# A two-layer transformer trunk: one more Strassen block in the last FFN, and six adaLN sums moved into FoX's head steps

## What is computed

```python
c_act = silu(c)
for i in range(2):
    mod = c_act @ ada_w[i] + ada_b[i]
    sh_a, sc_a, g_a, sh_f, sc_f, g_f = split(mod, 6)
    h = x * (1 + sc_a) + sh_a
    y = mla(h) if i == 0 else fox(h)           # 16 heads each, output projection w_o
    x = layer_norm(ALPHA * x + (1 + g_a) * y)
    h = x * (1 + sc_f) + sh_f
    y = (silu(h @ w1[i]) * (h @ w3[i])) @ w2[i]
    x = layer_norm(ALPHA * x + (1 + g_f) * y)
```

## Time and profile before

| | us |
|---|---|
| median of 3 runs | 2184.3 (2183.52 to 2187.05) |
| the profiled execution | 2183.23 |
| its span, first to last instruction | 2181.5 |
| PE busy | 2130.8 (98%) |
| DVE busy | 1677.3 (77%) |
| ACT busy | 1024.9 (47%) |
| mean granted clock of TensorE | 0.997 |

### The profile page before, as it was taken

The page is one execution under the profiler, slowest core; times in us unless marked ns, Lnnn a source line. Parts: engine busy times, 40 slices in busy tenths (PEclk is TensorE's granted clock), DMA queues, the critical chain, the costliest instruction groups (busy, mean ns, idle before and its releaser), DMA issues.

```text
span 2181.5 us, 25010 instructions
## 1 busy us (share of the span) xinstructions
PE 2130.8 (98%) x9515; PEld 1737.1 (80%) x9515; DVE 1677.3 (77%) x1868; ACT 1024.9 (47%) x1334; POOL 105.1 (5%) x208
## 2 busy tenths in 40 slices
PE   5799999999999999999999999999999999999999
PEld 2378877888888888888788888878888888888887
DVE  6789989787777777778887566878787755787766
ACT  1077636544443444443544454554445534465543
POOL 2101100000000000000000000000000000000000
PEclk9999999999999999999999999999999999999999
DMA  9999997789998898999678778958985765576672
GB/s 388 418 363 365 360 391 271 283 296 336 338 338 328 322 337 323 325 332 366 216 270 329 258 270 288 343 178 267 348 301 206 277 230 175 162 257 217 223 281 85
DMA packets 177065, 635.90 MB, mean 291 GB/s; under 512 B 20385, under 2 KB 51377, under 8 KB 150705
## 3 DMA queue, kind: packets, MB, share of 16 engines
q1 hardware_dynamic: 147298, 427.93, 54.6%
q0 software_dynamic: 27792, 201.34, 24.7%
q10 hardware_dynamic: 1856, 5.04, 0.6%
HBM read 616.37 MB, written 17.86 MB: 291 GB/s over the span
## 4 chain that ended last, share of the span: by engine, by line
PE 87%; DVE 6%; DMA 5%; ACT 1%; issue 1%; POOL 0%; ACTq 0%; SPq 0%; DVEq 0%; POOLq 0%
PE ps L2106 45%; PE ps L2112 22%; PE ps L2409 7%; PE ps L2415 3%; PE ps L2123 3%; DMA gate<-in_ada_w 3%; PE ps L2391 2%; DMA raw<-in_mla_w_o 1%; DVE wlo L1356 1%; PE ps L2396 1%; DMA ada_head<-in_ada_w 1%; DVE ada_w L1393 1%; DVE gate L1393 1%; DMA ada_w<-in_ada_w 1%; PE ps L2335 0%
## 5 line engine op out<-in xcount | busy, mean ns | idle before, releaser
L850 ACT ACTIVATE whi<-raw 128x1024 fp32r<-128x1024 f32 (+1 forms) x645 | 679.0, 1056 | 852.6 <-PE ps L2112 698.4
L1356 DVE TENSOR_TENSOR wlo<-raw,whi 128x1024 fp32r<-128x1024 f32 (+1 forms) x645 | 777.2, 1214 | 356.2 <-ACT whi L850 354.2
L2106 PE MATMUL ps<-whi,hT_hi 128*128 128x512 f32 x1432 | 447.8, 394 | 2.3 <-DVE hT_lo L1784 2.3
L2106 PE MATMUL ps<-whi,hT_lo 128*128 128x512 f32 x1432 | 441.7, 390 | 0.0
L2112 PE MATMUL ps<-wlo,hT_hi 128*128 128x512 f32 x1432 | 382.9, 389 | 0.0
L1393 DVE CUSTOM_DVE_ANT_0 ada_w<-ada_w,c_bc,cols 128x2048 f32<-128x2048 f32 x145 | 339.7, 2344 | 14.8 <-ACT c_bc L1224 8.5
L2106 PEld LDWEIGHTS ps<-whi,hT_lo 128*128 128x128 f32 x1432 | 268.8, 188 | 56.6
L2112 PEld LDWEIGHTS ps<-wlo,hT_hi 128*128 128x128 f32 x1432 | 268.8, 188 | 56.2
L2106 PEld LDWEIGHTS ps<-whi,hT_hi 128*128 128x128 f32 x1432 | 266.1, 188 | 56.1 <-DVE hT_lo L1784 2.9
L2106 PE MATMUL ps<-whi,uT_lo 128*128 128x512 f32 x656 | 201.9, 389 | 0.0
L2106 PE MATMUL ps<-whi,uT_hi 128*128 128x512 f32 x656 | 201.9, 389 | 0.0
(11 more groups left out here) (317 smaller groups left out, 2028.9 us busy)
## 6 DMA issues: line engine op xcount, KB each, us to landing
raw<-in_ffn_w SPq DMA_DIRECT2D x436, 512.0 KB, 5.6
ada_w<-in_ada_w POOLq DMA_DIRECT2D x145, 1024.0 KB, 8.1
raw<-in_fox_w_in SPq DMA_DIRECT2D x96, 512.0 KB, 5.3
raw_more<-in_ffn_w SPq DMA_DIRECT2D x92, 512.0 KB, 5.3
ada_head<-in_ada_w POOLq DMA_DIRECT2D x16, 1024.0 KB, 20.1
raw<-in_mla_w_o SPq DMA_DIRECT2D x32, 512.0 KB, 8.7
raw<-in_fox_w_o SPq DMA_DIRECT2D x32, 512.0 KB, 5.4
gate<-in_ada_w POOLq DMA_DIRECT2D x12, 1024.0 KB, 8.9
```

The costliest lines, as they stand in the source:

```text
L850: nc.scalar.activation(split_hi(pl.unit)[:, 0:n], raw_of(pl.unit)[:, 0:n], ACT.Copy).then_inc(hi_ready, 1)
L1356: nc.vector.tensor_tensor(split_lo(pl.unit)[:, 0:n], raw_of(pl.unit)[:, 0:n], split_hi(pl.unit)[:, 0:n].bitcast(F32), ALU.subtract).then_i ...
L2106: nc.tensor.matmul(ps[:, 2 * pair + t, 0:width], a[:, t * P:(t + 1) * P], w_hi, start=(first and c == 0 and a is hi), stop=False)
```

## The change

Fast are now the blocks 3 to 10, eight in place of seven. The mixing moves from block 3 to block 2. So that all sums are done by then, the limit of the sums in FoX goes from `ada_end(1, SH_F)` (176) to all 192, and the second sum of a head step is made in every even step, 0 to 18, where it was made in steps 2, 6, 10 and 14. The first sum stands in every step as before.

```diff
-FAST_FROM = 4
+FAST_FROM = 3
...
 def one_ada(i):
-    return i % 4 == 2 and i < H
+    return i % 2 == 0
...
                     if layer == 1 and i >= 4:
                         o_low(i - 4)
-                    if layer == 0 or pl.ada < ada_end(1, SH_F):
+                    if layer == 0 or pl.ada < len(ADA_ORDER):
                         ada()
                     gap(gaps[0])
...
-                    if layer == 0 and i < TICKS - 1 and i not in (0, 2, 4) or layer == 1 and one_ada(i) and pl.ada < ada_end(1, SH_F):
+                    if layer == 0 and i < TICKS - 1 and i not in (0, 2, 4) or layer == 1 and one_ada(i) and pl.ada < len(ADA_ORDER):
                         ada()
                     gap(gaps[1])
                     gap(gaps[2])
...
             def mix_inputs():
-                assert pl.ada == len(ADA_ORDER)
+                assert pl.ada == len(ADA_ORDER), pl.ada
...
             for k in range(FOX_F + 1, FOX_GROUP):
                 units(1)
-                if k % 4 == 3 and pl.ada < ada_end(1, SH_F):
+                if k % 4 == 3 and pl.ada < len(ADA_ORDER):
                     ada()
```

## The result

The changed kernel takes **2194.0 us** (median of 5 runs, 2190.9 to 2195.1); the kernel before takes 2184.7 (2183.5 to 2187.1). The ratio is 1.0038, 95% interval 1.0027 to 1.0048: slower by 9.3 us between the medians, where 5.5 were forecast. The profiled execution took 2192.5 us with a span of 2190.7, 9.2 more than before, so that it can be compared with the rows of before as it stands.

A forecast was written before the change was run, and what follows sets the result against it. TensorE, busy 98% of the span, was taken as the bound: 2181.5 - 1.4 (fast block) + 5.3 (idle) + 1.6 (clock) = 2187.0, plus 1.7 outside the span and 1.1 to the median: 2189.8 us, range 2184.5 to 2198.5.

The forecast's parts named there:

- The fast block, 1.4 us: Block 3 in the last FFN: 186 matmuls instead of 192, 42.15 us instead of 43.52, a gain of 1.4 us.
- Sums of steps 0, 4, 8 at nothing: Long head steps: some 18 us with DVE at 65% have room for each sum and its load; cost nothing.
- Step 12's new sum at nothing: First short head step: costs nothing by its own instruction, since step 14 has the same pair and PE does not stop.
- Step 18 reaches PE: Last head step: its second sum delays head 15's `o_low`, for which PE's projection unit 14 waits; 5.3 us idle.
- the last load starts when no other sum's is on its way: Load of step 18's second sum: given as a reason for the lower half of the idle time's bounds.
- Idle time 5.3 us: Before PE's projection unit 14: `o_low` 5.8 us late less 0.50 slack; bounds 1.8 and 12.8 us.
- The other formula, 5 x (2.66 + L) - 44.0: Steps 12 to 18: PE's delay from five links of 2.66 us plus load latency L; 5.8 us at 7.3, 12.8 at 8.7.
- The instruction alone, 1.8 us: Step 18's second sum with its data there: 2.27 us less 0.50 slack costs PE 1.8 us, the lower bound.
- The clock, 1.6 us: Behind the idle time at unit 14: lower granted clock adds 1.6 us of matmul, bounds 0 and 3.4.
- Only the instruction: Rival for step 18: loads land in 5 to 6 us, PE loses 1.8 us, clock unaffected; 2184.7 us, chance 0.20.
- Starved throughout: Rival for steps 12 to 18: load latency 8.7 us from step 12, delay 12.8 us; about 2197.3 us, chance 0.18.

The follow-up runs named there:

- experiment 11: Changed kernel with ten fast blocks (1 to 10), second sums in steps 0 to 11, third ones in 2, 4, 6, 8, 10, more in the projection: 2182.5 us, 0.9991.
- Experiment 2: Changed kernel with step 18's second sum made in step 1 instead: 2188.5 us, 1.0018 against the kernel before.
- experiment 5: Changed kernel with a quarter of the bytes in the loads of the nine sums from step 13 to step 18's second: 2185.5 us, 1.0000.
- experiment 3: Changed kernel with Strassen from block 4 on, as in the kernel before, so only the six sums are moved: 2196.5 us, 1.0050.
- experiment 7: Changed kernel with ACT's 1 MB copy of the gate row issued in head step 10 instead of step 16: 2192.5 us, 1.0032.
- experiment 1: Changed kernel with its ten second sums all in the long steps 0 to 9, none in steps 12 to 18: 2183.5 us, 0.9995.
- experiment 4: Kernel before with the second sum of step 14 made in step 18 instead: 2188.4 us, 1.0014.
- experiment 9: Kernel before with step 14's second sum made in step 18, plus 14 unused matmuls on PE ahead of unit 14: 2187.2 us, 1.0012.
- experiment 10: Changed kernel with nine fast blocks (2 to 10), second sums in steps 0 to 11 only and three more sums in the projection: 2182.6 us, 0.9994.
- experiment 6: Changed kernel with step 18's second sum made behind the low part of head 15, not ahead of it: 2189.2 us, 1.0019.
- experiment 8: Changed kernel with 20 unused matmuls on PE right ahead of output unit 14: 2191.6 us, 1.0035.

## Why the prediction was right, and where its sizes were off

- **The fast block, 1.4 us: right**, 43.52 to 42.16 us, no wait of PE around it.
- **Sums of steps 0, 4, 8 at nothing: right.** PE is busy 198.00 of 198.00 us, and even with 28 sums there in place of 14 (experiment 11) it still is.
- **Step 12's new sum at nothing: wrong by its load.** The step that failed is "cost nothing by its own instruction, since step 14 has the same pair of sums": true of the instruction, but its megabyte came on top. The loads issued at 1366.63 and 1370.43 took 8.1 and 8.8 us, where the kernel before has two, issued at 1369.24 and 1376.57, of 5.0. DVE entered step 16 at 1391.11, 2.1 us later than the 1389.03 of the earlier trace rows from which I reckoned. Experiment 2 shows it without step 18's sum (1390.34, 1.4 us later than before from step 12 on); with short loads DVE enters step 16 at 1389.13 (experiment 5), so the instruction by itself costs nothing there.
- **Step 18 reaches PE: right**, place, releaser and kind of cost. Predicted and measured starts: step 16's second sum 1393.0 and 1395.07, step 17's 1398.0 and 1399.43, 18's first 1404.0 and 1406.64, 18's second 1409.0 and 1411.27. All are late by 1.4 to 2.6 us, around the 2.1 with which DVE came in. On the chain that ended last, 9.2 for my 8.3 was nearly made up by 5.6 for my 6.3. Two readings there were wrong. That the last load starts when no other sum's is on its way fails by my own dates: it is issued at 1400.7, and the one before it lands at 1404.0 (measured, 1402.09 and 1406.6). And the steps 16 to 18 have five sums where three stood, not four.
- **Idle time 5.3 us: 6.9 measured**, within the bounds 1.8 and 12.8. The other formula, 5 x (2.66 + L) - 44.0, does well: the five latencies have a mean of 7.56, it gives 7.1. The median of the kernel before, 7.3, would have given 5.8; the rows of single loads, which I took, gave less because they were dated from the undisturbed kernel.
- **The instruction alone, 1.8 us: right**, 1.7 with short loads.
- **The clock, 1.6 us: 2.8 measured.** The mis-sized term with the second largest part. I took the shorter of two cases of the earlier trace rows while the idle time was longer than either of the earlier trace rows; the longer case, 3.4, was the nearer one.
- **Rivals.** Only the instruction: it needs L below 6.5, and three of five links had 8.8 or more. Starved throughout: its latency of 8.7 holds for three links of five, and the mean keeps it out; its sign, PE waiting for masks or scaled p in steps 13 to 16, shows in no profile. But PE waits for scaled p in step 17 in the experiments 2, 3 and 7 (0.5 to 1.6 us), and at the last pv in the changed kernel (1.06 us). The truth lies between the forecast and this rival. The 60 us in which the sums starved ran at 324 GB/s, while 4 us of the same trace reach 430 and experiment 11 holds 359 over 198 us: so what failed the sums looks to be the time of one load among others, with two buffers, and not the rate of the whole. A third buffer, which would tell, was not tried. The Trainium skill (DMA: Bandwidth & Descriptors, "Where 436 GB/s comes from") gives some 358 GB/s per core as the limit of loads from HBM. The 430 over 4 us speaks against it, as the 422 over 20 us did before. The 359 over 198 us, at a DMA share of 1.00, is no sign for it, since PE waited for nothing there.
- **Sum:** 1.6 more of idle time, 1.2 of clock, 0.4 of PE time in the short steps, 0.3 at the start of step 12 make 3.5 of the 3.7 us by which the span missed (9.2 for 5.5).

## What to carry to other kernels

Moving a step costs its load as well as its instruction, and it makes its neighbours' loads longer. Ask of a pair of buffers how far apart their users stand (here 2.66 us + latency per link) and sum the links through the whole stretch, with the latency of loads that stand as close as the new ones will, rather than date each load from a trace in which fewer were asked for. Busy shares do not tell where there is room: with DVE at 81% (experiment 11) the 18 us steps hid every sum, the 7.35 us steps, at 82% before the change, did not hide theirs. An idle time of TensorE is to be priced with the matmuls behind it. The row whose idle time is nearest in length is no safe price: it gave 1.6 us here (behind 3.97), where 2.8 were measured and the shorter idle time of the same rows (2.86) had 3.4.

## What was not expected of the hardware

- **A load's latency goes with its neighbours.** In the 60 us of the short steps a load of 1 MB lands in 5.0 to 9.2 us, 5.6 between two of 9.2, and that is no chance. In the short steps ahead of the gate copy, loads of which no other sum's is on its way at the same time take 5.0 to 6.0 us (the kernel before, experiments 1, 4, 9, 10 and 11). In the changed kernel those that share 1.0, 4.3, 5.3, 6.1 and 6.6 us of their time with others of their kind take 5.0, 6.9, 8.1, 8.8 and 9.2. A longer load also shares more by being longer; but experiment 4 took one such neighbour away, and 8.5 and 8.7 us became 5.1 and 5.0. It does not hold everywhere: in the last FFN of the kernel before a load takes 8.1 us with 0.8 us shared. A quarter of the bytes lands in 3.7 to 5.7 us (experiment 5).
- **What the clock does behind an idle time.** The longest idle times, of the profiles above, with the lowest granted clock in the 4 us windows behind: 1.68 us, 1.00; 2.28 (behind 1.90 and 1.64 in the 12 us before), 0.66; 3.26, 0.74; 3.81 (experiment 2), 0.54; 5.38 (experiment 6), 0.51; 5.84, 0.50. A window mixes the two levels: behind the 3.26 us too, matmuls start 0.43 us apart, half speed, for some 3.5 us. The price: 1.7 us behind 3.26, 2.8 us behind 5.84.
- **The place of a wait is not fixed.** Three kernels have the same program up to unit 14. The changed one was idle for 5.84 us ahead of it and 1.06 at the pv before; that of experiment 8 for 5.19 us at the pv; that of experiment 3 for 1.6, 3.5 and 4.2 us at the turns, the pv and unit 14. Each has one profile, so whether it differs from one execution of a program to the next is not shown (the changed kernel's times spread over 4.3 us, those of the kernel before over 3.5). The 6.9 us of idle time, and their parts above, are those of one execution.
